# A filler in front of block 2's activation buffers: 288 instead of 256 bytes behind the weights' home, modulo 512

## The reference

```
h = modulate(rmsnorm(s, norm_g), m, i)
gu = h @ w_in
y = (silu(gu[..., :D_FF]) * gu[..., D_FF:]) @ w_out
return s + 0.5 * gate(m, i) * y
```

## Time and profile before

| | us |
|---|---|
| median of 3 runs | 2667.72 (2667.08 to 2668.32) |
| span of the profiled execution | 2663.7 |
| TensorE busy (matmul) | 2571.9, 97% |
| TensorE weight loads | 2248.1, 84% |
| VectorE busy | 1481.6, 56% |
| ScalarE busy | 1028.1, 39% |

### The profile page before, as it was taken

The page is one execution under the profiler, slowest core; times in us unless marked ns, Lnnn a source line. Parts: engine busy times, 40 slices in busy tenths (PEclk is TensorE's granted clock), DMA queues, the critical chain, the costliest instruction groups (busy, mean ns, idle before and its releaser), DMA issues.

```text
span 2663.7 us, 47408 instructions
## 1 busy us (share of the span) xinstructions
PE 2571.9 (97%) x19893; PEld 2248.1 (84%) x19893; DVE 1481.6 (56%) x2149; ACT 1028.1 (39%) x1404; POOL 64.2 (2%) x80
## 2 busy tenths in 40 slices
PE   7999999999899999999999999999999999998999
PEld 6999999899899878888776678888788888866999
DVE  6877786777777653333525453333543333545655
ACT  4544564545466432222324432122332222444433
POOL 2004000000200000000000000000000000000000
PEclk9999999999999999999999999999999999999999
DMA  8578766657685652432436443332352433554573
GB/s 233 173 233 197 206 171 193 206 190 220 177 230 166 189 142 66 118 97 83 150 90 190 143 131 87 107 96 76 116 132 76 122 85 91 173 159 136 149 202 108
DMA packets 613845, 393.61 MB, mean 148 GB/s; under 512 B 47470, under 2 KB 609428, under 8 KB 613539
## 3 DMA queue, kind: packets, MB, share of 16 engines
q1 hardware_dynamic: 610623, 383.31, 49.7%
q0 software_dynamic: 2176, 6.42, 1.1%
q10 hardware_dynamic: 868, 1.31, 0.1%
HBM read 389.94 MB, written 1.05 MB: 147 GB/s over the span
## 4 chain that ended last, share of the span: by engine, by line
PE 89%; DVE 5%; ACT 3%; issue 1%; DVEq 1%; DMA 0%; ACTq 0%; SPq 0%
PE acc L946 12%; PE acc L947 12%; PE acc L948 12%; PE scores L946 6%; PE scores L947 6%; PE scores L948 6%; PE scores L989 3%; PE scores L990 3%; PE scores L991 3%; PE acc L989 3%; PE acc L991 3%; PE acc L990 3%; PE stat L1116 1%; ACT whi L1443 1%; DVE wlo L1966 1%
## 5 line engine op out<-in xcount | busy, mean ns | idle before, releaser
L1443 ACT ACTIVATE whi<-raw 128x2048 fp32r<-128x2048 f32 (+3 forms) x346 | 568.8, 1647 | 864.0 <-PE acc L948 266.5
L1966 DVE TENSOR_TENSOR wlo<-raw,whi 128x2048 fp32r<-128x2048 f32 (+2 forms) x306 | 630.1, 2059 | 221.7 <-ACT whi L1443 221.2
L946 PE MATMUL acc<-h_hi,whi 128*128 128x256 f32 (+1 forms) x2052 | 660.3, 322 | 11.8 <-DVE u L2510 3.5
L947 PE MATMUL acc<-h_lo,whi 128*128 128x256 f32 (+1 forms) x2052 | 652.3, 318 | 0.0
L948 PE MATMUL acc<-h_hi,wlo 128*128 128x256 f32 (+1 forms) x2052 | 652.1, 318 | 0.0
L946 PEld LDWEIGHTS acc<-h_hi,whi 128*128 128x128 f32 x2052 | 387.8, 189 | 50.3 <-issue 9.8
L947 PEld LDWEIGHTS acc<-h_lo,whi 128*128 128x128 f32 x2052 | 387.8, 189 | 28.5 <-issue 1.2
L948 PEld LDWEIGHTS acc<-h_hi,wlo 128*128 128x128 f32 x2052 | 387.8, 189 | 27.3
L946 PE MATMUL scores<-h_hi,whi 128*128 128x256 f32 (+1 forms) x960 | 318.9, 332 | 0.6 <-DVE wlo L1966 0.5
L947 PE MATMUL scores<-h_lo,whi 128*128 128x256 f32 (+1 forms) x960 | 317.9, 331 | 0.0
L948 PE MATMUL scores<-h_hi,wlo 128*128 128x256 f32 (+1 forms) x960 | 317.9, 331 | 0.0
(11 more groups left out here) (306 smaller groups left out, 3495.2 us busy)
## 6 DMA issues: line engine op xcount, KB each, us to landing
raw<-in_ffn_w_in_dram SPq DMA_DIRECT2D x176, 512.0 KB, 5.1
raw<-in_w_mod_dram SPq DMA_DIRECT2D x72, 1024.0 KB, 5.1
raw<-in_w_in_dram SPq DMA_DIRECT2D x62, 1024.0 KB, 5.8
raw<-in_w_up_dram SPq DMA_DIRECT2D x88, 512.0 KB, 5.1
raw<-in_ffn_w_out_dram SPq DMA_DIRECT2D x64, 704.0 KB, 4.6
raw<-in_w_down_dram SPq DMA_DIRECT2D x32, 704.0 KB, 4.6
raw<-in_w_out_dram SPq DMA_DIRECT2D x16, 1024.0 KB, 6.0
raw<-in_w_branch_dram SPq DMA_DIRECT2D x16, 512.0 KB, 7.0
```

Of the source, the lines that this page charges most:

```text
L946: pe.matmul(bank, wh, hi[:, c0 + k, 0:width], start=(k == 0), stop=False)
L947: pe.matmul(bank, wh, lo[:, c0 + k, 0:width], start=False, stop=False)
L1443: return act.activation(out_, in_, ACT.Copy, **kw)
L1966: dve.tensor_tensor(wlo[:, s % 2, 0:el], raw[:, slot, 0:el], f32(whi[:, s % 2, 0:el]), ALU.subtract).then_inc(s_lo, 1)
```

## The change

One number changes. `lead(288)` gives (288 - 256) mod 512 = 32 bytes, so `lead2` has 8 elements in place of 128. Modulo 512 the tiles behind it move up by 32 bytes; in absolute terms they move down by 480.

```diff
             xc = q("xc", [P, DC, SEQ])
-            q("lead2", lead(256))
+            q("lead2", lead(288))
             h2_hi = q("h2_hi", [P, DC, 512], F32R)
             h2_lo = q("h2_lo", [P, DC, 512], F32R)
```

## The result

The changed kernel takes 2698.2 us (median of 4 runs, 2696.1 to 2699.0) against 2667.4 for the one before (4 runs): ratio 1.0114, 95% interval 1.0102 to 1.0126. It is slower by 30.8 us; the prediction was 2646, in a range from 2641 to 2663. The profiled execution has a span of 2697.3 us (before: 2663.7). These are single executions, so their spans differ by 33.6 us where the medians differ by 30.8.

A forecast was written before the change was run, and what follows sets the result against it. The prediction took TensorE's matmul density as the bound: 16.4 us (512 columns) plus 6.3 (256 columns) less 0.9 returned in waits gives 21.8 us saved, from 2667.7 to 2645.9, say 2646; range 2641 to 2663.

The forecast's parts named there:

- the one on the matmuls of 512 columns: Block 2's 5454 matmuls of 512 columns: each saves 3.0 ns, as block 1's rate suggests, 16.4 us in all.
- Of three distances 256 is the worst: Split matmuls at 256 columns: distances 288, 256 and 224 modulo 512 have mean durations of 279, 283 and 281 ns.
- The bounds: Block 2's 512-column matmuls: 3.3 ns saved at best, 2.5 at block 1's slower rate, otherwise nothing or a 3 ns loss.
- TensorE's density sets the time: Whole kernel: TensorE busy 2571.9 of 2663.7 us, wait chain 89% TensorE; how densely matmuls follow each other sets the end.
- the rival of the row step: Block 2's rows 2048 bytes apart, against block 1's 1024, make the 8 cycles; nothing changes, 2667.7 us; chance 0.09.
- The term of -6.3 us: Block 2's 2094 matmuls of 256 columns: 120.0 to 117.0 ns, 3.0 ns less each, 6.3 us.
- what comes back: Block 2's 576 matmuls of first units: half of their 3.0 ns saving returns as longer waits for normalisation, 0.9 us.
- slower: long streams lose: Block 2's 512-column matmuls stall twice at distance 288, losing 3.0 ns each: +10.4 us in all, 2678.1 us; chance 0.10.
- The Trainium skill's rule that the prediction weighed: Loading next weights steals nothing from the running matmul, so distance has no price and time stays; given little weight.

The follow-up runs named there:

- the third sweep: Kernel of split matmuls alone, without the computation: 48 for each distance from 0 to 252 bytes in steps of 4, rising then falling; 226.7 to 240.0 ns at 512 columns.
- the first sweep: Kernel of split matmuls alone, without the computation: distances 0 to 496 in steps of 16, several widths; at 256 and 288, 120.0 and 116.6 ns (256 columns), 226.9 and 233.3 (512).
- the sweep with fixed rows: Second sweep of matmuls alone, here with the same activation row and slice each time: 120.0, 226.7 and 233.4 ns again.
- the half and quarter loads: Sweep settings loading 64 or 32 columns in place of 128; at distance 0, 113.3 and 117.8 ns (256 columns), 230.0 and 231.7 (512).

## Why the prediction was wrong

**The step that failed** is the one on the matmuls of 512 columns: "The excess is 32 cycles at both widths in block 2, and the weight load begins at the matmul's start in both, so I take block 1's saving." That one coincidence at distance 256 was the whole ground for carrying a number from one width to the other. The sweep shows that the excess depends on distance and width together, and 256 is a place where the widths happen to agree. At 288 the long stream has 48 cycles and not 24. The term was -16.4 us; 5454 x 6.7 ns is +36.4, and the trace has +35.3 for its 5397 undisturbed ones.

**"Of three distances 256 is the worst"** was true for 256 columns only. At 512 columns its place, 0 modulo 256, is the best of 64 in the third sweep, so any other filler would have lost there (240 gave 226.7 as well, but only in the first sweep).

**The bounds were too narrow.** I had written that the trace showed no 512-column matmul at this distance, and then bounded the loss by the size of the gain, 3 ns. No row gave that end. In the sweeps the long stream's cost goes from 226.7 to 240.0 ns over the distances, so the loss could have been 13 ns a matmul, 73 us in all.

**What held.** TensorE's density sets the time. The distance between the two operands is the cause, not the stage: the rival of the row step fell, since block 2's rows are still 2048 bytes apart at 116.7 ns, and also by the sweep with fixed rows. The 256-column matmuls went to 116.7 ns as forecast; the last feed-forward part alone is worth 4.0 us (1.6 to 6.7) where 1584 x 3.3 = 5.2 were due. The term of -6.3 us has -8.4 in the trace, of which the disturbed matmuls take back 3.8; the prediction had 0.9 for what comes back. Nothing else moved: 213.2 us of other matmuls for 212.6, and the same busy time on VectorE. The rival "slower: long streams lose" was the right mechanism with its place; its price of 3.0 ns was less than half of the measured 6.7, and with no row of that shape at that place a chance of 0.10 was low.

The Trainium skill's rule that the prediction weighed, in "TensorE: Matmul & The Clock Gate", section "Step-by-step: what each phase is for", that the load of the next tile steals nothing from the running matmul, fits bfloat16 here: 6 cycles of excess at all four distances, and the same page's N/2.4 + 2.5 ns gives the measured 215.8. It doesn't fit float32r at the upper level of the clock, with 16 to 64 cycles by distance and width.

**What stays open.** How the two reads meet, and whether a float32r stream without loads beside it would be free of the excess at 2.4 GHz. An excess in proportion to the loaded columns is ruled out by the half and quarter loads, and I have no model that gives the 64 values. Nor do I know what picks one of two patterns. At distance 192 in block 1 the trace has 10.0 us of stretches in the slower pattern (683.0 us, where 5940 x 113.3 ns is 673.0) and 6.5 us more in disturbed matmuls; why these grew I don't know.

## What to carry to other kernels

A price read at one shape is a price for that shape: where an excess comes from two activities that run beside each other, measure it at each width before it is carried over, and treat one agreement as one point. For float32r matmuls whose loads run beside the stream, at 2.4 GHz, the distance of the two operands modulo 256 bytes is worth a sweep of its own for each width, with a look for places that settle in two patterns; here 0 suits 512 columns and 112 suits 256, and giving each width its own place saved 22.6 us of 2667.7.

## What the runs showed of the hardware beyond that

- At 2.4 GHz float32r pays 16 to 64 cycles above its columns while loads run beside it. bfloat16 pays 6 (109.2 and 215.8 ns), and so does each of the two recorded halves of a plain float32 matmul (215.8 ns each for 256 columns, 6 above twice the columns), at the four distances tried.
- At 1.2 GHz float32r with loads beside it takes 213.3 and 426.7 ns, with no excess, at distances 256 and 288.
- The period is 256 bytes (tested in steps of 16), and 4 bytes matter: at 512 columns 226.7 ns at distance 0, 237.7 at 4.
- A lone float32r load takes 0.29 us where bfloat16 takes 0.10, both at the lower clock.
- Some places have two lasting paces (113.3 and 117.8 ns at 192) within one execution.
